# A two-part network in fp32 on one core: layer 0's leftover tiles in one stream with the output planes among its last head pairs, and the even layer's entry rearranged with the low parts of its weights made in halves

## Chip, cores, metric

One core of a Trainium2 chip runs the whole program. The metric is the device time of one execution in microseconds; lower is better.

## What is computed

The reference is a chain of four mixers and two MLPs on 512 tokens of width 1024, all in fp32. Two of the mixers matter here.

```python
def stick_breaking_layer(x, norm_g, w_in, w_out):          # layer 0
    q, k, v, gate = jnp.split(rms_norm(x, norm_g) @ w_in, 4, axis=-1)      # 16 heads of 64
    ...
        z = einsum(q, k) / 8;  mask = s < t
        log_fail = where(mask, log_sigmoid(-z), 0)
        later = cumsum(log_fail, reverse) - log_fail
        a = where(mask, exp(log_sigmoid(z) + later), 0)
    return x + (o * silu(gate)) @ w_out

def even_mixer(h, ...):                                    # the even layer
    qa, ka, va, qi, ki, wi, qb, kvb, gb = split_cols(h @ w_in, EVEN_SPLITS)
    # rope on qa, ka, qi, ki, qb and three of kvb
    o_a = dsa_attention(...)     # 8 heads, keys chosen by an index score (top 128 of up to 512)
    o_b = nsa_attention(...)     # 8 heads: compressed keys (gelu of two small products), selected, window; sigmoid gates
    return concat(o_a, o_b) @ w_out
```

Each matrix is multiplied nearly exactly: both operands are split in a high part (rounded to the fp32r type) and a low part (the rest), and a product is three matmuls, high by high, low by high and high by low.

## The kernel before

**Weights.** SyncE streams blocks of 128x1024 fp32 (512 KB) in the order of a list `plan` into two raw buffers WRAW; ScalarE makes the high part WH (`split_high`, line 252), VectorE or, for the blocks in `on_pool`, GpSimd the low part WL (`split_low`, line 261), in three buffers each (NR, NS = 2, 3). The load of block b (line 243) waits for the low part of block b-2. The high part of block b waits for that load and for the last matmul on block b-3. In the even layer, the blocks in question are in the order e5, wc2(0), wc1(1,2), e6, wc1(1,3), e7, e8, wc2(1), e9, e10, e11, ..., e14, and then e_o; `E_Q` is 7. `split("e", t)` on an engine means the block three places behind e_t: e7 gives e9, e8 gives e10, wc2(1) gives e11, e9 gives e12.

**A tile** is eight "eighths", each of three matmuls of 512 columns (`three`, lines 275 to 277), with its result in one of eight banks of PSUM.

**Layer 0** (`l0_tensor`, `l0_vector`, `l0_scalar`, `l0_gpsimd`) makes gates and values, then the first tiles q0, k0, q1 (`l0_first`), and then goes through eight pairs of heads m. For a pair: `logits(m)` (lines 614 and 620), `values(m-1)` (line 642), eight eighths of tile k(m+1), `sums(2m)` (line 629), four eighths of q(m+2), `sums(2m+1)`, four more. The chain of a head is logits on TensorE; Abs, Exp, Ln on ScalarE (`soft`, lines 775 to 781); `fails` on VectorE (lines 714, 719); `fail_low` on GpSimd (line 822); sums on TensorE; `weigh` on ScalarE (line 787); values. A tile q or k is evicted by VectorE (696), rounded (705), and its low part is GpSimd's (812). The result of a pair goes through `gated` on VectorE (727), `og_zero` on ScalarE (792) and `og_low_zero` on GpSimd (828), and is then an operand of the output product `out_sets`, one "plane" (three matmuls, an eighth of an output tile) per pair. In pair 6 there is one tile left (k7) and in pair 7 none; six planes of output tile 0 stand there before `sums(14)`, one after it, seven planes of tile 1 after `sums(15)`, seven of tile 2 after `values(7)`.

**The even layer** (`l2_tensor`, `l2_vector`, `l2_scalar`, `l2_gpsimd`) makes its first tiles and the compressed keys (the entry) and then goes through 56 steps. In step s TensorE does `turn(s-4)` (line 1607, or 1602 for a compressed unit), `values(s-5)` (1626), `scores(s)` (1583, 1590), perhaps a rotation for rope (1487), and some eighths of the remaining tiles e9 to e14; VectorE does `maxima(s-1)` (1805), `recips(s-3)`, rope, `taken` (eviction, 1726), and rounds of the top-k (`e_rounds`, 1701 and 1703); ScalarE does `copied(s-4)`, `exps(s-1)` (2019), the query's high part (2005) and high parts of weights; GpSimd does `scale(s-3)` (2144), the query's low part `low` (2132), rope's cosine `cos` (2100), and low parts of weights. `scores(s)` needs the banks that `exps(s-2)` frees, `turn(s-4)` needs `scale(s-4)` and banks 4 and 5. Where a tile ends is set by a table of eighths per step, `E_FILL`, that starts in step 2:

```python
        E_FILL0, E_FILL = 2, (1, 2, 1, 1, 2, 1, 0)
        def e_eighths(step):
            s = step - E_FILL0
            return E_FILL[s % 7] if 0 <= s < 42 else 0
```

The order of each engine is that of the code; there is no scheduler.

Of the kernel before, what the change touches and what calls it, by code (L numbers as in the profile page):

```python
# [133 lines left out]
def program(nc, A, out):  # L134
    ctx = ExitStack()
    with ctx:
# [117 lines left out]
        def split_low(e, w, b, pool):  # L254
# [3 lines left out]
            if b >= NS:  # L258
# [3 lines left out]
                            ALU.subtract).then_inc(*inc("s_low_pool" if pool else "s_low", ("low", b)))  # L262

# [307 lines left out]
        l0_first = [("l0q", 0), ("l0k", 0), ("l0q", 1)]  # L571
        l0_beside = [[("l0k", m + 1)] * (m < 7) + [("l0q", m + 2)] * (m < 6) for m in range(8)]

        def l0_tensor(e, w):
# [7 lines left out]
            for name, m in l0_first:  # L582
                tile_t(e, w, name, m, h_hi, h_lo, need)
            w.wait_ge(*at("const", 3))

            def linear(name, m):
# [3 lines left out]
                bank, was = banks.hold((name, m), 7, ("evac", name, m))  # L590
# [4 lines left out]
                for k in range(KT):  # L595
# [4 lines left out]
                    yield  # L600

# [33 lines left out]
            def values(m):  # L635
                o, was = banks.hold(("l0 out", m), 6, ("gated", m))
# [9 lines left out]
            for m in range(8):  # L646
                logits(m)
                if m:
                    values(m - 1)
                tiles = [linear(*t) for t in l0_beside[m]] + [iter(())] * 2  # L650
                if m == 7:
                    out_sets(e, w, "l0o", 0, 0, range(0, 6), 7)
                for _ in range(8):
                    next(tiles[0], None)
                sums(2 * m)
                if m == 7:
                    out_sets(e, w, "l0o", 0, 0, range(6, 7))
                for _ in range(4):
                    next(tiles[1], None)
                sums(2 * m + 1)  # L660
                for _ in range(4):
                    next(tiles[1], None)
            out_sets(e, w, "l0o", 0, 1, range(0, 7), 0)
            values(7)
            out_sets(e, w, "l0o", 0, 2, range(0, 7), 1)
            for m in range(3):
                out_sets(e, w, "l0o", 0, m, [7])
# [3 lines left out]
        def l0_vector(e, w):  # L671
# [27 lines left out]
            def high(name, m):  # L699
# [7 lines left out]
                split_low(e, w, after_block(name, m), False)  # L707
# [13 lines left out]
            def gated(m):  # L721
# [5 lines left out]
                e.tensor_tensor(TMP[:, m % 2, :], BANK[6][:, :], l0g[:, m, :], ALU.mult).then_inc(  # L727
                    *inc("s_gated", ("gated", m)))
            for t in l0_first:
                evicted(*t)  # L730
                high(*t)
            for m in range(8):
                fails(2 * m)
                fails(2 * m + 1, [0])
                beside = l0_beside[m]
# [3 lines left out]
                if m:  # L739
                    gated(m - 1)  # L740
                if len(beside) > 0:
                    high(*beside[0])
                if len(beside) > 1:
                    evicted(*beside[1])
                    high(*beside[1])
            gated(7)
# [2317 lines left out]
```

## Time and profile before

| | us |
|---|---|
| median of 3 runs | 1934.42 (1933.19 to 1934.52) |
| the profiled execution's own time | 1929.6 |
| its span, from the first to the last instruction | 1927.8 |
| TensorE busy in the span | 1847.4 (96%) |
| VectorE, ScalarE, GpSimd busy | 968.3, 796.8, 468.9 |
| mean granted TensorE clock | 0.99 |

Times in rows are from the span's start. "[1.59 <-POOL LH L822]" at the end of a row means that the engine had been idle for 1.59 us and what it waited for last. PEclk is the granted share of TensorE's clock: 1.00 is 2.4 GHz, 0.50 is 1.2 GHz.

### The profile page before, as it was taken

The page shows a single profiled execution, that of the slowest core. Times are in us where ns is not written, and L with a number is a line of the kernel's source. Part 1 is how long each engine was busy: PE and PEld are TensorE (multiplying, and loading weights), DVE is VectorE, ACT ScalarE, POOL GpSimd, SP SyncE. Part 2 cuts the span into 40 slices and gives each one's busy share as a digit, 9 for nine tenths or more (in the row PEclk, how much of TensorE's full clock was granted, in tenths as well). Part 3 has the DMA queues.
Part 4 walks back from the last instruction along what each step waited for, and adds up shares of the span by engine and source line. Part 5 has one row for each costly group of instructions (what it writes and reads, how often), then busy time and mean ns, then how long its engine had stood idle before and what let it go on. Part 6 is the DMA issues. An engine that isn't in the chain of part 4 may idle for free.

```text
span 1927.8 us, 24564 instructions
## 1 busy us (share of the span) xinstructions
PE 1847.4 (96%) x9682; PEld 1452.9 (75%) x9682; DVE 968.3 (50%) x1574; ACT 796.8 (41%) x1401; POOL 468.9 (24%) x467
## 2 busy tenths in 40 slices
PE   6999998999999989999999999999999999999997
PEld 5987776766677746667888888877888788888885
DVE  5355554575545587843543333355555654333334
ACT  4235664355435345554442323133444544232322
POOL 0025551011312125541120102005556312010200
PEclk9999999999999989999999999999999999999998
DMA  4321111221012410001233232322211123323331
GB/s 154 99 77 44 55 45 45 87 77 44 23 45 95 127 55 23 23 23 36 90 105 99 88 98 95 99 79 77 66 55 58 48 94 99 98 88 99 98 99 66
DMA packets 40289, 143.32 MB, mean 74 GB/s; under 512 B 4592, under 2 KB 4976, under 8 KB 40176
## 3 DMA queue, kind: packets, MB, share of 16 engines
q1 hardware_dynamic: 40176, 141.76, 22.7%
q8 instruction: 78, 1.28, 0.3%
q14 instruction: 35, 0.29, 0.0%
HBM read 139.64 MB, written 2.10 MB: 74 GB/s over the span
## 4 chain that ended last, share of the span: by engine, by line
PE 86%; DVE 5%; ACT 4%; POOL 3%; issue 1%; DMA 1%; DVEq 0%; SPq 0%; POOLq 0%; ACTq 0%
PE BANK L275 22%; PE BANK L277 22%; PE BANK L276 22%; PE BANK L856 2%; PE BANK L629 2%; PE BANK L1626 2%; PE BANK L1583 1%; PE BANK L1607 1%; PE BANK L2403 1%; DVE LH L719 1%; PE BANK L913 1%; PE BANK L614 1%; PE BANK L2378 1%; DVE SCR L714 1%; ACT WH L252 1%
## 5 line engine op out<-in xcount | busy, mean ns | idle before, releaser
L252 ACT ACTIVATE WH<-WRAW 128x1024 fp32r<-128x1024 f32 x262 | 273.5, 1045 | 494.9 <-PE BANK L277 458.2
L261 DVE TENSOR_TENSOR WL<-WRAW,WH 128x1024 fp32r<-128x1024 f32 (+1 forms) x249 | 324.9, 1305 | 260.4 <-ACT WH L252 260.2
L275 PE MATMUL BANK<-HH,WH 128*128 128x512 f32 x1048 | 426.9, 407 | 21.1 <-DVE WL L261 18.1
L277 PE MATMUL BANK<-HL,WH 128*128 128x512 f32 x1048 | 410.5, 392 | 0.0
L276 PE MATMUL BANK<-HH,WL 128*128 128x512 f32 x1048 | 410.1, 391 | 0.0
L275 PEld LDWEIGHTS BANK<-HH,WH 128*128 128x128 f32 x1048 | 197.9, 189 | 71.5 <-ACT WH L252 18.8
L276 PEld LDWEIGHTS BANK<-HH,WL 128*128 128x128 f32 x1048 | 198.2, 189 | 43.2 <-issue 5.3
L277 PEld LDWEIGHTS BANK<-HL,WH 128*128 128x128 f32 x1048 | 197.9, 189 | 42.8
L2253 POOL TENSOR_TENSOR HID<-TMP,HID 128x512 fp32r<-128x512 f32 x64 | 83.0, 1297 | 534.2 <-ACT HID L2234 534.2
L277 PE MATMUL BANK<-HID,WH 128*128 128x512 f32 x512 | 202.3, 395 | 0.0
L275 PE MATMUL BANK<-HID,WH 128*128 128x512 f32 x512 | 202.2, 395 | 0.0
L276 PE MATMUL BANK<-HID,WL 128*128 128x512 f32 x512 | 202.2, 395 | 0.0
L463 DVE TENSOR_TENSOR X<-X,BANK 128x512 f32<-128x512 f32 x96 | 66.1, 688 | 251.2 <-PE BANK L277 251.2
L2230 ACT ACTIVATE TMP<-TMP 128x512 f32<-128x512 f32 x64 | 40.5, 632 | 202.8 <-DVE TMP L2207 202.8
L277 PEld LDWEIGHTS BANK<-HID,WH 128*128 128x128 f32 x512 | 96.1, 188 | 23.3
L275 PEld LDWEIGHTS BANK<-HID,WH 128*128 128x128 f32 x512 | 96.1, 188 | 23.3
L276 PEld LDWEIGHTS BANK<-HID,WL 128*128 128x128 f32 x512 | 96.1, 188 | 23.3
L2207 DVE SCALAR_TENSOR_TENSOR TMP<-BANK,RS 128x512 f32<-128x512 f32 x64 | 44.1, 689 | 59.4 <-PE BANK L277 59.4
L812 POOL TENSOR_TENSOR L0P<-TMP,L0P 128x512 fp32r<-128x512 f32 x16 | 36.4, 2276 | 152.6 <-DVE L0P L705 152.6
L822 POOL TENSOR_TENSOR LH<-SCR,LH 128x512 fp32r<-128x512 f32 (+1 forms) x48 | 53.2, 1107 | 45.9 <-DVE LH L719 45.9
L2019 ACT ACTIVATE SCR<-BANK,ST 128x512 f32<-128x512 f32 (+3 forms) x96 | 49.7, 527 | 17.7 <-DVE ST L1805 17.5
L2658 ACT ACTIVATE SCR<-BANK,ST 128x128 f32<-128x128 f32 (+3 forms) x64 | 33.2, 523 | 56.9 <-DVE ST L2529 56.9
(400 smaller groups left out, 3137.5 us busy)
## 6 DMA issues: line engine op xcount, KB each, us to landing
WRAW<-in_w SPq DMA_DIRECT2D x77, 512.0 KB, 3.4
WRAW<-in_wu SPq DMA_DIRECT2D x64, 512.0 KB, 3.3
WRAW<-in_wd SPq DMA_DIRECT2D x64, 512.0 KB, 3.3
WRAW<-in_w0o SPq DMA_DIRECT2D x8, 512.0 KB, 3.5
WRAW<-in_w1o SPq DMA_DIRECT2D x8, 512.0 KB, 3.4
WRAW<-in_wc SPq DMA_DIRECT2D x8, 512.0 KB, 3.4
WRAW<-in_w2o SPq DMA_DIRECT2D x8, 512.0 KB, 3.3
WRAW<-in_w3o SPq DMA_DIRECT2D x8, 512.0 KB, 3.3
```

The lines of the kernel that those rows point to most:

```text
L252: e.activation(WH[b % NS][:, 0:n], WRAW[b % NR][:, 0:n], ACT.Copy).then_inc(*inc("s_high", ("high", b)))
L261: e.tensor_tensor(WL[b % NS][:, 0:n], WRAW[b % NR][:, 0:n], WH[b % NS][:, 0:n].bitcast(F32), ALU.subtract).then_inc(*inc("s_low_pool" if p ...
L275: e.matmul(dst, ah, bh, start=first and i == 0, stop=False)
L276: e.matmul(dst, al, bh, start=False, stop=False)
L277: made = e.matmul(dst, ah, bl, start=False, stop=last and i == len(sets) - 1)
L463: e.tensor_tensor(X[:, m, :], X[:, m, :], banks[name, m], ALU.add).then_inc(*inc("s_evac", ("evac", name, m)))
L629: made = e.matmul(l0_bank(h, bk)[:, c0 + 128 * (jj - j):c0 + size[j]], ntri if jj == j else nones, nlf[:, h % 2, col[jj]:col[jj] + size[jj ...
L822: e.tensor_tensor(LH1[:, h % 2, c], l0_buf[h % 3][:, c], LH0[:, h % 2, c].bitcast(F32), ALU.subtract).then_inc(*inc("s_fail_lo", ("fail lo ...
L2019: e.activation(e_exp(u)[:, b, 0:n], BANK[2 * (u % 2) + b][:, 0:n], ACT.Exp, bias=e_stat(u, b), accum_out=e_stat(u, 2 + b)).then_inc(*inc(" ...
L2207: e.scalar_tensor_tensor(out=TMP[:, t % 4, :], in0=banks[("up", L, c), m], scalar=0.0, in1=RS[:, :], op0=ALU.max, op1=ALU.mult).then_inc(* ...
L2230: e.activation(t, t, ACT.Square).then_inc(*inc("s_hid", ("hid square", L, c, m)))
L2253: e.tensor_tensor(lo[:, m, :], TMP[:, (8 * c + m) % 4, :], hi[:, m, :].bitcast(F32), ALU.subtract).then_inc(*inc("s_hid_lo", ("hid lo", L, ...
```

## The change

In layer 0, q1 is no longer among the first tiles. The tiles from q1 on are one stream of 112 eighths: four before `logits(0)`, twelve in pair 0 before `sums(0)` and eight in the other pairs, and again four after each `sums` (not in pair 6). The output planes start in pair 6 (two after each `sums`), go on in pair 7 with eight before `sums(14)`, two before and two after `sums(15)`, and five after `values(7)`. q1 goes to bank 7, k1 to bank 6, `values(7)` to bank 0, output tiles 0, 1, 2 to banks 7, 6, 1. `gated(6)` and `og_zero(6)` come earlier (before `fails(14)`, and between `soft(14)` and `soft(15)`), `og_low_zero(6)` between `fail_low(14)` and `fail_low(15)`, and the low part of the last pair's result is VectorE's. In the even layer's entry, gelu and the sigmoid of the gates come earlier on ScalarE, rope earlier on VectorE, the low parts of e9, e10 and e11 later there (after `taken(E_Q + 1)`, in step 4 and in step 5), `second(1)` and `c_values` earlier on TensorE. The rope of tile e8 moves from steps 1 and 2 to steps 3 and 4 on VectorE, and no rounds of the top-k are done in steps 0 to 2. The table of eighths starts in step 1 and rests in step 22. In the steps the low part of a block (e12 to e14, e_o 0 to 2) is made by GpSimd in two halves, two and three steps after the tile's end instead of in that step.

```diff
+        def split_low_half(e, w, b, half):
+            n = stream[b][2] // 2
+            c = slice(n * half, n * half + n)
+            w.wait_ge(*at("used", b - NS))
+            w.wait_ge(*at("high", b))
+            e.tensor_tensor(WL[b % NS][:, c], WRAW[b % NR][:, c], WH[b % NS][:, c].bitcast(F32),
+                            ALU.subtract).then_inc(*inc("s_low_pool", ("low", b) if half else ("low half", b)))
...
-        l0_first = [("l0q", 0), ("l0k", 0), ("l0q", 1)]
+        l0_first = [("l0q", 0), ("l0k", 0)]
...
+            tiles = (part for t in [("l0q", 1)] + [t for beside in l0_beside for t in beside] for part in linear(*t))
...
-            for m in range(8):
+            eighths(4)
+            for m in range(6):
                 logits(m)
                 if m:
                     values(m - 1)
-                tiles = [linear(*t) for t in l0_beside[m]] + [iter(())] * 2
-                if m == 7:
-                    out_sets(e, w, "l0o", 0, 0, range(0, 6), 7)
-                for _ in range(8):
-                    next(tiles[0], None)
+                eighths(8 if m else 12)
                 sums(2 * m)
-                if m == 7:
-                    out_sets(e, w, "l0o", 0, 0, range(6, 7))
-                for _ in range(4):
-                    next(tiles[1], None)
+                eighths(4)
                 sums(2 * m + 1)
-                for _ in range(4):
-                    next(tiles[1], None)
-            out_sets(e, w, "l0o", 0, 1, range(0, 7), 0)
+                eighths(4)
+            logits(6)
+            values(5)
+            eighths(8)
+            sums(12)
+            planes(0, 0, 1)
+            sums(13)
+            planes(0, 2, 3)
+            logits(7)
+            values(6)
+            planes(0, 4, 5)
+            planes(1, 0, 1, 2, 3, 4, 5)
+            sums(14)
+            planes(0, 6)
+            planes(1, 6)
+            sums(15)
+            planes(2, 0, 1)
             values(7)
-            out_sets(e, w, "l0o", 0, 2, range(0, 7), 1)
+            planes(2, 2, 3, 4, 5, 6)
...
-        E_FILL0, E_FILL = 2, (1, 2, 1, 1, 2, 1, 0)
+        E_FILL, E_REST = (1, 2, 1, 1, 2, 1, 0), 22
+        def e_place(step):
+            return step - 1 - (step >= E_REST)
...
-            return E_Q + 1 if step == 1 else e_ended(step - 1)
+            return E_Q + 1 if step == 3 else e_ended(step - 1)
...
                 if k == 2:
                     rot_of(E_Q)
-            second(1)
+                if k == 4:
+                    second(1)
+            c_values()
...
             taken(E_Q)
+            after_rope(E_KW)
+            after_rope(E_Q)
+            keys(1)
+            c_keys(1)
+            taken(E_Q + 1)
             split("e", E_Q)
-            after_rope(E_KW)
-            keys(1)
-            after_rope(E_Q)
-            taken(E_Q + 1)
-            split("e", E_Q + 1)
-            c_keys(1)
-            split("wc2", 1)
...
-                if step == 1:
+                if step == 2:
                     index_sum(3)
-                if step == 2:
+                if step == 3:
                     c_values()
+                if step == 4:
+                    split("e", E_Q + 1)
+                if step == 5:
+                    split("wc2", 1)
...
-                for _ in range(1 if busy or step % 2 else 2):
+                for _ in range(0 if step < 3 else 1 if busy or step % 2 else 2):
...
             split("e", E_Q)
-            keys(1)
-            high(E_Q)
             gelu(1)
             e.activation(gates, gates, ACT.Sigmoid).then_inc(*inc("s_gates", ("gates",)))
             e.preload_act_table_set("natural_log_exp_and_others")
+            keys(1)
+            high(E_Q)
+            swapped(1)
             split("e", E_Q + 1)
             split("wc2", 1)
...
-                if e_ended(step) is not None:
-                    split("e", e_ended(step))
+                for half in range(2):
+                    if e_ended(step - 2 - half) is not None:
+                        split_low_half(e, w, block["e", e_ended(step - 2 - half)] + NS, half)
```

The order of instructions moves at these three places. Lines of the changed program differ from those of the one before; the names are the same.

TensorE in pair 6 of layer 0, where `sums(12)` ends and `sums(13)` begins (LH0 and LH1 are the high and low parts of a head's log terms, OG0H and OG0L those of a pair's gated result); before:

```order
L629 MATMUL BANK<-LH0,TRI 128x128
L629 MATMUL BANK<-LH1,TRI 128x128
L629 MATMUL BANK<-LH0,TRI 128x512 [waits s_fail_lo]
L629 MATMUL BANK<-LH1,TRI 128x512
L629 MATMUL BANK<-LH0,TRI 128x384
```

and now:

```order
L643 MATMUL BANK<-LH0,TRI 128x128
L643 MATMUL BANK<-LH1,TRI 128x128
L284 MATMUL BANK<-OG0H,WH2 128x512 [waits s_og_hi,s_evac,s_og_lo,s_low,s_high]
L285 MATMUL BANK<-OG0H,WL2 128x512
L286 MATMUL BANK<-OG0L,WH2 128x512
L284 MATMUL BANK<-OG0H,WH2 128x512 [waits s_og_lo,s_og_hi]
L285 MATMUL BANK<-OG0H,WL2 128x512
L286 MATMUL BANK<-OG0L,WH2 128x512
L643 MATMUL BANK<-LH0,TRI 128x512 [waits s_fail_lo]
L643 MATMUL BANK<-LH1,TRI 128x512
```

Two planes of output tile 0 now stand between the sums of the two heads.

VectorE at the even layer's entry, from `taken(E_Q)` on (WL1<-WRAW0,WH1 is the low part of e9, WL2<-WRAW1 of e10, WL0<-WRAW0 of e11; ekcT is the compressed keys' copy); before:

```order
L1726 SCALAR_TENSOR_TENSOR TMP<-BANK,RS 128x512 [waits s_tile]
L261 TENSOR_TENSOR WL1<-WRAW0,WH1 128x1024 [waits s_high]
L1738 TENSOR_TENSOR TMP<-BANK,ROPE 128x512 [waits s_roped,s_rot]
L1745 TENSOR_TENSOR TMP<-TMP 128x512 [waits s_cos,s_sin]
L1761 TENSOR_TENSOR ekw<-TMP,ekw 128x512 [waits s_key_high]
L1738 TENSOR_TENSOR TMP<-BANK,ROPE 128x512 [waits s_roped,s_rot]
L1745 TENSOR_TENSOR TMP<-TMP 128x512 [waits s_cos,s_sin]
L1726 SCALAR_TENSOR_TENSOR TMP<-BANK,RS 128x512 [waits s_tile]
L261 TENSOR_TENSOR WL2<-WRAW1,WH2 128x1024 [waits s_high]
L1770 COPY ekcT<-BANK 128x62 [waits s_tile]
L261 TENSOR_TENSOR WL0<-WRAW0,WH0 128x1024 [waits s_high]
```

and now:

```order
L1785 TENSOR_TENSOR TMP<-BANK,ROPE 128x512 [waits s_roped,s_rot]
L1792 TENSOR_TENSOR TMP<-TMP 128x512 [waits s_cos,s_sin]
L1785 TENSOR_TENSOR TMP<-BANK,ROPE 128x512 [waits s_roped,s_rot]
L1792 TENSOR_TENSOR TMP<-TMP 128x512 [waits s_cos,s_sin]
L1808 TENSOR_TENSOR ekw<-TMP,ekw 128x512 [waits s_key_high]
L1817 COPY ekcT<-BANK 128x62 [waits s_tile]
L1773 SCALAR_TENSOR_TENSOR TMP<-BANK,RS 128x512 [waits s_tile]
L261 TENSOR_TENSOR WL1<-WRAW0,WH1 128x1024 [waits s_high]
L1852 TENSOR_REDUCE ST<-BANK 128x2 [waits s_scores] x2
```

The low part of e9 moved from the head of this stretch to its end, and the row maxima of steps 1 and 2 follow it at once.

GpSimd around the end of tile e9 in the steps (WL1<-WRAW1,WH1 is the low part of e12); before:

```order
L2144 TENSOR_SCALAR SCR<-SCR,ST,enat 128x256
L261 TENSOR_TENSOR WL1<-WRAW1,WH1 128x1024 [waits s_high,s_tile]
L2144 TENSOR_SCALAR SCR<-SCR,ST,enat 128x384 [waits s_recip]
L2144 TENSOR_SCALAR SCR<-SCR,ST,enat 128x384
L2100 TENSOR_TENSOR TMP<-TMP,ROPE 128x512 [waits s_rot]
```

and now:

```order
L2153 TENSOR_TENSOR TMP<-TMP,ROPE 128x512 [waits s_rot]
L2197 TENSOR_SCALAR SCR<-SCR,ST,enat 128x384 [waits s_recip]
L2197 TENSOR_SCALAR SCR<-SCR,ST,enat 128x384
L2185 TENSOR_TENSOR EQ<-TMP,EQ 128x512 [waits s_query]
L270 TENSOR_TENSOR WL1<-WRAW1,WH1 128x512 [waits s_high,s_tile]
L2197 TENSOR_SCALAR SCR<-SCR,ST,enat 128x128 [waits s_recip]
L2197 TENSOR_SCALAR SCR<-SCR,ST,enat 128x128
L270 TENSOR_TENSOR WL1<-WRAW1,WH1 128x512
```

The low part stood ahead of the cosine; it now comes behind the query's low part, in two pieces with a unit's scaling between them.

## Rows read from the trace of the kernel before

**Rows 1.** The page: its first line.
```profile
span 1927.8 us, 24564 instructions
```
**Rows 2.** Windows: us; busy (instructions) of PE, PEld, DVE, ACT, POOL; PEclk; DMA; GB/s.
```profile
113.00:128.00 15.00, 15.00 (x67) 12.39 (x66) 5.93 (x8) 2.78 (x3) 4.58 (x2) 1.00 0.28 87
300.52:303.93 3.41, 2.88 (x7) 2.42 (x8) 0.00 (x0) 0.29 (x2) 0.39 (x1) 0.50 0.00 0
699.88:716.94 17.06, 11.67 (x45) 6.61 (x42) 14.35 (x35) 6.39 (x15) 3.20 (x3) 0.50 0.19 62
717.20:906.00 188.80, 177.19 (x1454) 127.40 (x1454) 112.15 (x265) 101.15 (x263) 84.82 (x113) 0.99 0.06 18
809.10:812.50 3.40, 3.40 (x26) 2.57 (x24) 3.37 (x8) 1.39 (x4) 0.66 (x1) 0.50 0.23 92
```
**Rows 3.** Waits of PE, 275 to 322 us: total, times, longest.
```profile
PE BANK L629 <- POOL LH L822: 3.2, 3, 1.6
PE BANK L275 <- POOL OG0L L828: 3.2, 1, 3.2
PE BANK L614 <- ACT SCR L787: 1.8, 1, 1.8
```
**Rows 4.** Timeline of PE in layer 0: start, duration, instruction [idle before].
```profile
129.93 2.20 PE L614 MATMUL BANK<-L0P 64*128 64x512 f32 x24 [1.09 <-DVE TMP L696]
141.01 2.99 PE L629 MATMUL BANK<-LH,TRI 128*128 128x512 f32 x20 [2.79 <-POOL LH L822]
```
**Rows 5.** Timeline of POOL and DVE in layer 0.
```profile
124.67 2.29 POOL L812 TENSOR_TENSOR L0P<-TMP,L0P 128x512 fp32r<-128x512 f32 x1 [3.15 <-DVE L0P L705]
...
290.40 0.43 DVE L719 CAST LH<-SCR 128x512 fp32r<-128x512 f32 x1
...
291.46 1.03 DVE L719 CAST LH<-SCR 128x512 fp32r<-128x512 f32 x1
...
298.38 0.73 POOL L822 TENSOR_TENSOR LH<-SCR,LH 128x256 fp32r<-128x256 f32 x1 [0.23 <-DVE LH L719]
299.64 1.26 POOL L828 TENSOR_TENSOR OG0L<-TMP,OG0H 128x512 fp32r<-128x512 f32 x1 [0.53 <-ACT OG0H L792]
```
**Rows 6.** Waits of PE at the even layer's entry, 687 to 717.2 us.
```profile
PE BANK L275 <- POOL EHL L2124: 1.8, 1, 1.8
...
PE BANK L1487 <- DVE TMP L1738: 0.6, 1, 0.6
```
**Rows 7.** Timeline of PE there.
```profile
708.87 1.33 PE L1583 MATMUL BANK<-eks,EQ 64*128 64x384 f32 x6 [4.51 <-ACT SCR L2019]
...
717.19 1.31 PE L1607 MATMUL BANK<-CF,SCR 128*128 128x128 f32 x8
```
**Rows 8.** Timeline of DVE and ACT there.
```profile
696.46 0.69 DVE L1726 SCALAR_TENSOR_TENSOR TMP<-BANK,RS 128x512 f32<-128x512 f32 x1 [0.22 <-PE BANK L277]
701.79 1.23 DVE L261 TENSOR_TENSOR WL<-WRAW,WH 128x1024 fp32r<-128x1024 f32 x1 [4.64 <-ACT WH L252]
...
706.03 1.22 DVE L1805 TENSOR_REDUCE ST<-BANK 128x2 f32<-128x1024 f32 x1
...
700.70 2.00 ACT L252 ACTIVATE WH<-WRAW 128x1024 fp32r<-128x1024 f32 x2
```
**Rows 9.** The weight loads of line 243, 690 to 710 us: issue to landing.
```profile
DMA to landing us min/median/max: 3.5/3.5/5.3
```
**Rows 10.** Waits of PE in the steps, 717.2 to 906 us.
```profile
PE BANK L1607 <- POOL SCR L2144: 6.7, 8, 1.7
PE BANK L1602 <- DVE SCR L1841: 2.7, 1, 2.7
```
**Rows 11.** Timeline of POOL in the steps.
```profile
755.20 2.35 POOL L261 TENSOR_TENSOR WL<-WRAW,WH 128x1024 fp32r<-128x1024 f32 x1 [1.68 <-ACT WH L252]
```
**Rows 12.** Groups of DVE's instructions by line, 717.2 to 906 us: busy, mean ns.
```profile
L1701 DVE MAX8 ST<-esc 128x8 f32<-128x384 f32 (+2 forms) x33 | 20.1, 610 | 0.2
L1703 DVE MATCH_REPLACE8 esc<-ST,esc 128x384 f32<-128x384 f32 (+2 forms) x33 | 19.9, 603 | 0.0
```

More of the change, by code:

```diff
@@ L583, in l0_tensor @@
                 tile_t(e, w, name, m, h_hi, h_lo, need)
+            banks.i += 1
             w.wait_ge(*at("const", 3))
@@ L589, in linear @@
                 wh, wl = (x[b % NS][:, 0:BW].rearrange("p (k n) -> p k n", k=KT) for x in (WH, WL))
-                bank, was = banks.hold((name, m), 7, ("evac", name, m))
+                bank, was = banks.hold((name, m), 6 if (name, m) == ("l0k", 1) else 7, ("evac", name, m))
                 w.wait_ge(*at("high", b))
@@ L600, in linear, with planes @@
                     yield
+            def planes(m, *ks):
+                for k in ks:
+                    out_sets(e, w, "l0o", 0, m, [k], (7, 6, 1)[m])
             def logits(m):
@@ L635, in values @@
             def values(m):
-                o, was = banks.hold(("l0 out", m), 6, ("gated", m))
+                o, was = banks.hold(("l0 out", m), 0 if m == 7 else 6, ("gated", m))
                 for key in was:
@@ L645, in values, with eighths @@
                 made.then_inc(*inc("s_o", ("o", m)))
-            for m in range(8):
+            tiles = (part for t in [("l0q", 1)] + [t for beside in l0_beside for t in beside] for part in linear(*t))
+            def eighths(n):
+                for _ in range(n):
+                    next(tiles)
+            eighths(4)
+            for m in range(6):
                 logits(m)
@@ L731, in l0_vector @@
                 high(*t)
+                split_low(e, w, after_block(*t), False)
+            evicted("l0q", 1)
+            high("l0q", 1)
             for m in range(8):
+                beside = l0_beside[m]
+                if m == 7:
+                    gated(6)
                 fails(2 * m)
                 fails(2 * m + 1, [0])
-                beside = l0_beside[m]
                 if len(beside) > 0:
@@ L1671, in l2_tensor @@
                     scores(step)
-                if e_turning(step) is not None:
+                if step == 1:
+                    rot_of(E_Q + 1)
+                elif step > 3 and e_turning(step) is not None:
                     rot_of(e_turning(step), (7,))
-                if step == 2:
-                    c_values()
                 for _ in range(e_eighths(step)):
@@ L2065, in l2_scalar @@
             keys(0)
+            swapped(0)
             split("wc1", 1, 3)
```

48 lines of the change are left out of this document (27 added, 21 removed).

## The prediction, made before the changed kernel ran

> **What bounds the kernel now.** I read the page first. The span is 1927.8 us [rows 1] and TensorE is busy in 96% of it, so it is TensorE's order that sets the end, and the change adds and removes no product. Time can come only from TensorE's waits and from stretches in which its granted clock is halved. Second, I took TensorE's waits by what ended them, in the three stretches whose order changes. From 275 to 302 us the reader sees three chains end last: the sums wait for GpSimd's low part of the log terms (3.2 us in 3 waits), the output planes for its low part of the gated result (3.2), the logits for `weigh` on ScalarE (1.8) [rows 3]. Two more stand at the start of layer 0: 1.09 before `logits(0)` and 2.79 before `sums(0)` [rows 4]. At the even layer's entry it waits 1.8 for gelu's low part and 0.6 for the rotated query [rows 6], then 4.51 for `exps(0)` [rows 7]; in the steps 6.7 for `scale` and 2.7 for a chain on VectorE [rows 10]. Third, windows show the clock. It is 0.50 in three stretches of 3.41, 17.06 and 3.40 us, where TensorE is busy 2.88, 11.67 and 3.40; half of each is lost, so 1.4, 5.8 and 1.7 us [rows 2]. In that table 67 matmuls fill 15.00 us at full clock, 0.224 each, so an eighth or a plane is 0.68. The stakes are these waits and losses, some 31 us, in a program whose other 1895 stand as they are.
>
> **Layer 0, its start: 2.6 us saved.** Before, k0's tile ended and 24 matmuls of q1 (5.4 us) covered its eviction, rounding and low part; 1.09 of it stood open. Now 12 cover it (2.7). k0's low part begins at 124.67 and takes 2.29 [rows 5], to 126.97, while TensorE, by its pitch, runs out near 126.0, so `logits(0)` waits about 1.0. `sums(0)` came 11.08 us after the start of `logits(0)` (141.01 less 129.93, [rows 4]), which is the length of that head's chain; 2.20 of logits and now 36 matmuls (8.1) instead of 24 stand beside it, 10.3, with small gaps 10.8, and I take 0.3 of wait. Waits go from 3.88 to 1.3. The splits that move behind `soft(1)` and `fails(1)` are wanted a pair later and cost nothing; without that pair of cover they would cost a low part of GpSimd, 2.29.
>
> **Layer 0, its end: 7.3 us saved.** The waits are 3.2, 3.2 and 1.8 [rows 3]; of the first, 0.3 belongs to `sums(12)` and stays, so 7.9 are at stake. Two planes (1.36) now stand before `sums(13)` and cover its 1.3. Twelve matmuls more before `values(6)` and `sums(14)` leave, I estimate, 0.4 and 0.2 of the 1.8 and 1.6. The 3.2 before the planes of pair 6 goes: `og_low(6)` is made early and planes of other pairs stand ahead. New waits come instead. `sums(15)` needs a low part that ended at 299.11 (298.38 and 0.73 [rows 5]); now `og_zero` stands ahead on ScalarE and `og_low` (1.26 [rows 5]) on GpSimd, and the casts of VectorE take 1.03 rather than 0.43 beside GpSimd's work [rows 5]; I take 300.3 and 1.1 of wait, and 0.3 at `values(7)`. That leaves 2.0, so 5.9 are saved. With no wait of 3.2 the stretch at half clock behind it goes, 1.4.
>
> **The even layer's entry: 8.0 us saved, 6 to 10.** Times here are on the scale of before, without what layer 0 saves. The low part of e9 leaves VectorE's path before the rope, so the wait of 0.6 for the rotated query goes; gelu comes before the keys on ScalarE, so the 1.8 goes too [rows 6]. Tile e8 then ends near 696.3 and `scores(0)` can start about 2 us earlier. But the low part of e9 now follows e8's eviction (0.69 [rows 8]): it runs from 697.0 to 698.3 (1.23 [rows 8]). The load of e11 goes into the buffer that this low part frees, so it is issued at 698.3 and lands 3.5 later [rows 9], at 701.8; its high part (2.00 for two, so 1.0 [rows 8]) stands ahead of `exps(0)` on ScalarE. Hence `exps(0)` near 702.9. Before, it followed the maxima that ended at 707.25 (706.03 and 1.22 [rows 8]), and `scores(2)` came 1.6 later, at 708.87 [rows 7]; now it comes at 704.5. TensorE idles about 3.6 before it, one wait where there were four. From 708.87 to `turn(0)` at 717.19 [rows 7] are 8.3, 0.9 of them idle, 7.4 busy at half clock: 3.7 at full. I add 1.7 for one stretch of half clock of the size of the one at 809.10 [rows 2], which gives `turn(0)` at 709.9, 7.3 earlier, with one eighth (0.7) more behind it: 8.0. The ends: if e11 lands at once, 10; if it takes the 5.3 of the slowest load [rows 9], 6.
>
> On whether the new wait halves the clock, rows do not agree: after the wait of 2.79 at 141.01 [rows 4] no half stretch stands in the trace, after the 2.7 near 809 [rows 10] one does [rows 2]. The Trainium skill (TensorE: Matmul & The Clock Gate, on the HAM clock gate) says that the gate looks at the engine in a rhythm of its own, not the program's; by that the 1.7 that I add is a throw, and the sum would be 25.1 without it.
>
> **The steps: 5.5 us saved, 0 to 11.** Here 6.7 and 2.7 us of waits [rows 10] and 1.7 of clock are at stake, 11.1. GpSimd waited 1.68 for the block's high part and then worked 2.35 on the whole low part [rows 11], with `scale` and the cosine queued behind. The halves come two and three steps later, when the high part is long made, and take about half each (nearest row: a GpSimd operation of 128x512 at 1.26 [rows 5]); by rows the two are 2.5, 0.2 dearer than the whole. Loads of later blocks wait two to three steps more, some 7 to 10 us, and have the rest of a tile as cover. What is late next: from a rotation's end the chain cosine (1.3), roped (0.7), high (0.65), query's low (1.3), a half (1.3) and scale (up to 1.5) is 6.7 us, against two steps of 3.4 each (188.80 over 56 [rows 2]). That is a tie, so some waits stay. VectorE is the other doubt: a round is 0.61 and 0.60 and small parts, about 1.4 us [rows 12], and those of steps 0 to 2, some five, are done later, beside the low parts of e10 and e11 (1.2 each) in steps 4 and 5. I take the middle of nothing and all, 5.5; a loss is the rival below.
>
> **The sum.** 2.6 + 7.3 + 8.0 + 5.5 = 23.4. The profiled execution took 1929.6, so 1906.2; the median of the runs is 1934.42, 4.8 above it, so 1911.0.
>
> **The rivals.** All on the median's scale; 0.2% of it, 3.9 us, is about what a measurement of this kernel can tell from no change.
>
> *More is gained.* The clock stays full at the entry (1.7) and all waits of the steps go (5.6 more): 30.7, 1903.7. For it: 2.79 of wait once left the clock alone. Against: the tie on GpSimd. Chance 0.12.
>
> *VectorE's later rounds take the gain of the steps.* Five rounds and two low parts are 9.6 us of VectorE moved into steps in which it also frees banks; if they cost the 5.5, 1916.5. For it: the 2.7 near 809 came from VectorE's chain [rows 10]. Against: VectorE is busy 112 of 188.80 us [rows 2]. Chance 0.11.
>
> *The halves stand in the way.* The 5.5 are not saved, and in two of six tiles a half (1.3) delays `scale` besides: 8.1 less, 1919.1. Chance 0.06.
>
> *The entry gains nothing.* The load of e11 and what follows it hold `exps(0)` until 707 or a later bank is late: 8.0 and a bit less, 1919.0 at the nearest. Chance 0.06.
>
> *It doesn't do what it says,* or several shortfalls meet, and it stays within 0.2%. Chance 0.04.
>
> *Slower.* The clock falls in the new wait of 3.6 at the entry and does not rise in the steps, whose matmuls are short and broken by waits. Each busy us at half clock costs half of itself; to undo 23.4 and 3.9 more it must be half for 55 us (27.3 by 2), which gives 1938.3. Before, the longest such stretch here was 17.06, with waits of 4.51 and 0.9 inside it [rows 2, 7]; the point from which it decides is three times that. Chance 0.03.
>
> **How the numbers follow.** The forecast has 0.58 and a range of its own of 1906 to 1916, from 6 to 10 at the entry and from 2 to 9 in the steps. To 1903.5 below and 1921 above the range takes in all rivals but the last two and leaves out some of the forecast's tails. Faster by over 0.2%: 0.93; within: 0.04; slower: 0.03.
>
> **What would show it right or wrong.** In layer 0: waits of about 1.0 and 0.3 before `logits(0)` and `sums(0)`, no wait over 0.5 before `sums(15)`, about 1.1 there, and clock 1.00 throughout. At the entry: one wait of 3 to 4 us before `scores(2)`, ended by `exps(0)`, with a high part that waited for a load just ahead of it on ScalarE; `turn(0)` 7.3 us earlier than before, besides the 9.9 of layer 0, so near 700 us. In the steps: `turn` waits for `scale` between 0 and 4 us in all, and none of `scores` for VectorE. I am wrong if `exps(0)` waits for the maxima again, if the half clock lasts beyond 7 us, or if new waits of over 1 us on evictions or maxima stand in the first ten steps.

## The result, and the profile after

The changed kernel takes 1916.38 us, the median of 4 runs (1915.41 to 1919.55), beside 1933.81 (1928.79 to 1934.52) for the kernel before, whose three runs have a fourth beside them here. The ratio is 0.9918, interval 0.9898 to 0.9939: some 16 us faster, or 0.8%. The forecast was 1911.0, with a range of 1903.5 to 1921. The profiled execution took 1915.41 and its span is 1913.6, against 1929.6 and 1927.8 [rows 1], so the traces differ by 14.2 us. Layer 0 and the entry came out close to their terms; the steps, which were to give 5.5, lost 1.6.

The page's first lines:

```profile
span 1913.6 us, 24565 instructions
## 1 busy us (share of the span) xinstructions
PE 1842.6 (96%) x9678; PEld 1450.0 (76%) x9682; DVE 967.3 (51%) x1575; ACT 796.1 (42%) x1401; POOL 471.0 (25%) x472
```

**Layer 0.** Waits of TensorE from 275 to 313.5 us, beside [rows 3]:

```profile
PE BANK L643 <- POOL LH L862: 1.3, 2, 1.1
PE BANK L284 <- DVE WL L261: 1.2, 1, 1.2
PE BANK L628 <- ACT SCR L823: 0.3, 1, 0.3
```

The 3.2 before pair 6's planes is gone. Of the sums' waits those of 1.31 and 1.59 are gone and one of 1.05 has come, before `sums(15)`; 0.22 stands before `sums(14)`. The 0.33 before `sums(12)` is as it was, but ends at 273.11, just outside this window, where it was inside before. The 1.8 before the logits is 0.3. The 1.2 on a weight's low part stood there before too, at 321.61 us of the old trace; it ends at 312.48 now, so 9.1 us are won by then. The two waits at the start, from the timeline of TensorE, beside [rows 4]:

```profile
126.91 0.51 PE L628 MATMUL BANK<-L0P 64*128 64x512 f32 x2 [0.97 <-POOL L0P L852]
139.38 0.50 PE L643 MATMUL BANK<-LH,TRI 128*128 128x512 f32 x1 [1.45 <-POOL LH L862]
```

The first is as forecast (1.0), the second is 1.45 where 0.3 was expected.

**The entry.** ScalarE's timeline shows what holds `exps(0)` (its first row is L2070), and TensorE's the wait for it:

```profile
687.90 1.06 ACT L252 ACTIVATE WH<-WRAW 128x1024 fp32r<-128x1024 f32 x1
691.92 1.06 ACT L252 ACTIVATE WH<-WRAW 128x1024 fp32r<-128x1024 f32 x1 [2.96 <-DMA WRAW<-in_w]
692.88 0.67 ACT L2070 ACTIVATE SCR<-BANK,ST 128x512 f32<-128x512 f32 x1
```
```profile
694.45 0.44 PE L1628 MATMUL BANK<-eks,EQ 64*128 64x384 f32 x2 [3.60 <-ACT SCR L2070]
699.74 0.27 PE L1652 MATMUL BANK<-CF,SCR 128*128 128x128 f32 x1
```

ScalarE idled 2.96 us for the load of e11 with its high part, and `exps(0)` stood behind it. `turn(0)` comes 387.26 us after layer 0's last wait; before, it was 395.58 (717.19 less 321.61), so 8.3 are won on this way. Some 0.7 of it is not the entry's: a wait of 1.28 at 652.12 of the old trace, ahead of the entry, is 0.58 here, and it is absent in the run below that has the old code there.

**The steps and the clock.** Waits of TensorE from `turn(0)` to just before the exit, beside [rows 10], and windows over the stage and over the two stretches at half clock that are left between the start and the end of the program (columns as in [rows 2]):

```profile
PE BANK L1652 <- POOL SCR L2197: 8.4, 7, 2.5
PE BANK L1647 <- DVE SCR L1888: 2.0, 1, 2.0
PE BANK L1652 <- ACT EPB L2086: 1.2, 2, 1.0
PE BANK L1632 <- issue: 0.6, 4, 0.2
PE BANK L1652 <- ACT MORE L2086: 0.3, 1, 0.3
```
```profile
696.00:699.41 3.41, 3.41 (x14) 2.29 (x14) 3.15 (x12) 1.23 (x4) 2.70 (x3) 0.50 0.01 2
699.70:889.60 189.90, 175.10 (x1446) 124.88 (x1448) 117.16 (x279) 100.20 (x262) 88.48 (x119) 1.00 0.07 23
890.57:893.98 3.41, 3.41 (x9) 2.63 (x8) 3.32 (x5) 2.11 (x4) 0.00 (x0) 0.50 0.68 244
```

From `turn(0)` to the output product are 189.8 us, with no us at half clock; before they were 188.3, of which 1.7 was lost to the clock. The waits grew from 9.0 to 11.7 (those over 0.28 us each). By the table of eighths, one eighth (0.7) of the stage's work now comes ahead of `turn(0)`, so at equal work the steps lost some 2.3. The second stretch follows the wait of 1.78 at the exit, which stood there before without one: 1.7 more. The account of the two spans: 9.1 and 8.3 won, 1.6 and 1.7 given back, 14.1 of 14.2.

### The profile page after: what moved, and what is told of

It reads as the page before. It is cut to its first block, busy times and chain, and to the rows that moved or that the text cites. A ratio compares the mean times of both kernels' runs of the same rounds, so it can differ in the third digit from the quotient of the medians.

```text
span 1913.6 us, 24565 instructions
## 1 busy us (share of the span) xinstructions
PE 1842.6 (96%) x9678; PEld 1450.0 (76%) x9682; DVE 967.3 (51%) x1575; ACT 796.1 (42%) x1401; POOL 471.0 (25%) x472
## 3 DMA queue, kind: packets, MB, share of 16 engines
q8 instruction: 78, 1.28, 0.3%
## 4 chain that ended last, share of the span: by engine, by line
PE 87%; DVE 5%; ACT 3%; POOL 3%; issue 2%; DMA 1%; DVEq 0%; SPq 0%; POOLq 0%; ACTq 0%
PE BANK L284 22%; PE BANK L286 22%; PE BANK L285 22%; PE BANK L897 2%; PE BANK L643 2%; PE BANK L1652 1%; PE BANK L1671 1%; PE BANK L1628 1%; PE BANK L2454 1%; PE BANK L954 1%; PE BANK L628 1%; PE BANK L2429 1%; DVE LH L745 1%; POOL LH L862 1%; DVE WL L261 1%
## 5 line engine op out<-in xcount | busy, mean ns | idle before, releaser
L2197 POOL TENSOR_SCALAR SCR<-SCR,ST,enat 128x512 f32<-128x512 f32 (+3 forms) x64 | 41.1, 651 | 61.9 <-DVE ST L1874 61.7
```

The lines of the kernel that those rows point to most:

```text
L2197: e.tensor_scalar(x, x, e_stat(u, 4 + b), gate, ALU.mult, ALU.mult).then_inc(*inc("s_scaled", ("e scaled", u, b)))
```

## The experiments

Three theories stood against each other for the steps. The forecast's own: the low part of the weights on GpSimd makes turn wait, and halving it helps. The second: the halves stand in the way where they are put. The third: other moves of the change (VectorE's rounds, the table of eighths) took the gain. For each run I compare the stage from `turn(0)` to the exit by its idle time (TensorE's waits over 0.28 us, without the exit's own 1.8) and by its time at half clock, since the second changes the time by more than most edits do.

**Layer 0 alone** (`l0_only`): all of the diff up to layer 0's end on the kernel before.

> The kernel before with the layer 0 part of the change alone. In the changed kernel's profile the last wait of layer 0 ends 9.1 us earlier than before (312.5 against 321.6). Theory (the parts are independent): the same waits as in the changed kernel (about 1.0 before logits(0), 1.4 before sums(0), 1.1 before sums(15)), the even layer as before (a wait of 4.5 before scores(2), turn(0) 395.6 after that last wait), so the span falls by 9 us. Rival (the even layer's waits depend on when its loads come): the entry or the steps change by more than 2 us although their code is that of before.

Measured: 1920.03 median (ratio 0.9945, 0.9928 to 0.9962), span 1916.8, 11.0 less than before. Layer 0's last wait ends at 312.75. The steps take 188.27 us, as before, with the same seven waits, the two largest of them 2.7 and 1.7. From layer 0's last wait to `turn(0)` it took 394.38 rather than 395.58: the wait of 1.28 at 652.12 of the old trace is not there. The parts are independent to about 1 us, less than the 2 that the rival asked for; the rest of the change gives the other 3 to 5.

**The low part whole, at the tile's end** (`low_whole`), **and whole, two steps later** (`low_whole_late`):

```diff
-                for half in range(2):
-                    if e_ended(step - 2 - half) is not None:
-                        split_low_half(e, w, block["e", e_ended(step - 2 - half)] + NS, half)
+                if e_ended(step) is not None:
+                    split("e", e_ended(step))
```

The second run has `e_ended(step - 2)` in both new lines.

> The changed kernel, but GpSimd makes each low part of e12 to e_o whole, in the step in which the tile ends, as before. Theory 1 (the halves help, and something else took the gain of the steps): the stage from turn(0) to the exit, 189.8 us in the changed kernel, gets longer by 2 to 4 us, with waits of turn for scale of 0.7 to 1.7 just behind each tile's end, and the span grows as much. Rival (the halves are what stands in the way, since each comes just ahead of a scale): the stage gets shorter by 1 to 4 us, and the wait of 2.5 (850.75) goes.

> The changed kernel, but the low part is made whole two steps after the tile's end. It tells the moving from the halving. If the moving alone helps, the stage from turn(0) to the exit is within 1 us of that of the changed kernel (189.8). If halving is what matters, each of six low parts of 2.35 us stands ahead of a scale, about 1.1 us more than a half does, and the stage gets longer by 3 to 7 us, with waits of turn for scale of 2 to 3.5. If the halves are in the way only by their number, the stage gets shorter.

Measured: 1920.23 (0.9944, 0.9929 to 0.9959) and 1920.85 (0.9950, 0.9935 to 0.9965). Idle in the steps was 12.5 and 15.1 against 11.7 in the changed kernel; the time at half clock there 17.1 and 13.7 us against none. With `low_whole` the wait of 2.5 at 850.75 goes, as its rival said, but others of 0.6 to 1.8 come at the tiles' ends, as its theory said; neither had the net of 0.8 more idle. Halves at this place thus save 0.8 of waits against the old form and 3.4 against a whole low part at the same place. It looked as if halving mattered; the next two runs say otherwise. Waits in the steps with the whole low part two steps later:

```profile
PE BANK L1652 <- POOL SCR L2197: 11.8, 9, 3.6
```

**The halves one step later** (`halves_34`): `step - 3 - half` in place of `step - 2 - half`. **The whole low part at three steps** (`whole_3`): `split("e", e_ended(step - 3))`.

> The changed kernel, but the two halves of a low part come three and four steps after the tile's end, not two and three. Theory (a half stands ahead of a unit's scale in the same step in which the query's low part is made, so turn waits there: 1.6 at 770.9 and 2.5 at 850.8): those two fall by 0.4 and 1.2 or more, no wait is added elsewhere, and the idle time of the steps falls from 11.7 to about 10. Rival (the blocks' loads and high parts come a step later and the next tile waits for its weights, or the half meets another late scale): waits of a tile's first product for a weight appear, or the idle time of the steps stays within 0.5 of 11.7.

> The changed kernel with the low part made whole three steps after the tile's end. It tells halving from placing, beside the kernel with halves at three and four steps (idle 9.3 in the steps) and that with the whole low part at two (15.1). If the place is what matters, the idle time is 9 to 10.5. If halving matters at any place, since 2.35 us stand ahead of a scale that is already due, it is 11.5 to 15, with waits of 1.5 to 2.5 three steps behind the tiles' ends.

Measured: 1910.30 (0.9886, 0.9858 to 0.9913) and 1911.72 (0.9894, 0.9880 to 0.9909), both below the changed kernel's 1916.38, though the intervals of the ratios still touch its own (0.9898 to 0.9939); the waits are clearer. GpSimd's timeline about the longest wait, first in the changed kernel, then with the halves one step later:

```profile
847.55 1.27 POOL L2185 TENSOR_TENSOR EQ<-TMP,EQ 128x512 fp32r<-128x512 f32 x1 [2.31 <-ACT EQ L2056]
848.78 1.26 POOL L270 TENSOR_TENSOR WL<-WRAW,WH 128x512 fp32r<-128x512 f32 x1
850.02 1.15 POOL L2197 TENSOR_SCALAR SCR<-SCR,ST 128x384 f32<-128x384 f32 x2
```
```profile
846.40 1.27 POOL L2185 TENSOR_TENSOR EQ<-TMP,EQ 128x512 fp32r<-128x512 f32 x1 [2.31 <-ACT EQ L2056]
847.65 1.14 POOL L2197 TENSOR_SCALAR SCR<-SCR,ST 128x384 f32<-128x384 f32 x2
```

The query's low part came late, since ScalarE's high part did; the half (L270) behind it pushed the scale (L2197) 1.26 further, and TensorE's wait was 2.49 instead of 1.27. The waits in the steps are the same with halves and with the whole, here of `halves_34` and `whole_3`:

```profile
PE BANK L1652 <- POOL SCR L2197: 6.0, 7, 1.3
PE BANK L1647 <- DVE SCR L1888: 2.0, 1, 2.0
```
```profile
PE BANK L1652 <- POOL SCR L2197: 6.0, 7, 1.3
PE BANK L1647 <- DVE SCR L1888: 2.0, 1, 2.0
```

Idle is 9.3 in both. So the place is what matters: halving is worth 3.4 at two steps, where a half or a whole stands ahead of a late scale, and nothing at three.

**The high part of e11 behind `exps(0)`** (`high_later`):

```diff
             split("e", E_Q + 1)
-            split("wc2", 1)
...
                     exps(step - 1)
+                if step == 1:
+                    split("wc2", 1)
```

> The changed kernel, but on ScalarE the high part of e11 comes in step 1 behind exps(0), not ahead of step 0. Theory (exps(0) waits for the load of e11 only because that high part stands ahead of it): maxima(0) ended at 689.8, so exps(0) starts at about 690 instead of 692.9, the wait of 3.6 before scores(2) falls to 0.7 or less, no half clock follows (1.7), turn(0) comes 4 to 4.6 earlier. Rival (the next wait takes its place: recips, the second bank, or exps(1) behind the high part, which still waits for the load until 691.9): turn(0) comes less than 2 us earlier, with a new wait of PE within the first three steps. The steps behind are either shifted as they are, or take up to 2 us back.

Measured: 1913.47 (0.9908, 0.9893 to 0.9923). `exps(0)` starts at 688.76, the wait before `scores(2)` is 0.58 and not 3.60, no half clock follows, and `turn(0)` comes 383.00 after layer 0's last wait, 4.3 earlier. That part is as the theory said. Two waits of 0.94 and 1.08 for `turn` came in the first steps, and 13.7 us at half clock stood in the stage: one stretch just behind the wait of 1.6 that ends at 767.07 and one from inside the wait of 2.5 that ends at 849.74, both of which had left the clock alone in the changed kernel. The two stretches here (only 0.6 us of waiting is inside), then two windows as long about the same waits in the changed kernel (3.4 us of waiting inside):

```profile
767.20:774.00 6.80, 6.80 (x30) 4.86 (x31) 3.38 (x9) 2.07 (x6) 3.76 (x6) 0.50 0.24 81
849.10:855.90 6.80, 6.17 (x25) 4.27 (x25) 1.03 (x2) 1.51 (x5) 4.04 (x7) 0.50 0.24 81
```
```profile
767.00:773.80 6.80, 5.16 (x45) 3.50 (x42) 6.20 (x16) 3.45 (x11) 6.23 (x8) 1.00 0.03 8
849.00:855.80 6.80, 5.05 (x44) 3.60 (x45) 1.03 (x2) 2.93 (x10) 5.65 (x8) 1.00 0.26 82
```

TensorE issued 55 matmuls here and 89 there in as much time, though it waited longer there. 13.7 us at half clock cost 6.8 at the most; the clock, and the two new waits, took what the entry gave, and the span is only 0.9 shorter. The ratio does not tell this run from the changed kernel; the gain shows in the trace alone.

**The table of eighths as before** (`table_two`): `return step - 2` in place of `return step - 1 - (step >= E_REST)`. **The rounds put back** (`rounds_early`): the 0 rounds of steps 0 to 2 become two, one, two.

> The changed kernel with the table of eighths started in step 2 and without the rest in step 22, as before (the halves still come two and three steps after a tile's end). Theory (the shift put a closing unit, whose result ScalarE copies out, and a rotation into one step without eighths: waits of 1.0 on the exponents' copy at 766 and 1.6 behind it): those two fall to the 0.8 to 1.5 that stood in that place before, and the idle time of the steps falls by 1 to 2 us. Rival (the shift was worth its price): waits of 1 us or more appear in the first ten steps or near 743, and the idle time stays or grows.

> The changed kernel with the top-k rounds of steps 0 to 2 put back (two, one and two). Theory (VectorE's later rounds delay the maxima and so recips, which scale then waits for: 1.2 at 740.8, 0.7 at 762.2, 1.0 at 797.1): turn(0) comes 1 to 3 us later, and the idle time of the steps falls by 1.5 to 3 us. Rival (the rounds are short against a step wherever they stand, and those waits come from the order cosine, low part, maxima itself): the steps' waits stay within 0.5 us of 11.7 and only the entry is later.

Measured: 1913.80 (0.9905, 0.9872 to 0.9938) and 1919.38 (0.9930, 0.9902 to 0.9958). With the old table idle in the steps is 10.0 instead of 11.7 (the 1.0 and 1.6 near 766 become 0.8; two of 0.65 appear early), as the theory said, but the entry's wait is 4.28 and not 3.60, since an eighth that covered it is gone. The two together are 14.3 with the old table and 15.3 with the new, so the shift mostly moves waits and costs 1.0. With the rounds put back idle in the steps is 13.2 and `turn(0)` comes 0.6 later, not 1 to 3: new waits of 0.6 and 1.2 stand at the start, and of the three blamed on late rounds none is shorter (1.20, 0.93 and 1.01 for 1.2, 0.7 and 1.0); only the 0.6 at 807, which was not among them, went. That theory falls, and so does its rival, which had the steps unchanged.

**q1's eviction behind `fails(0)`** (`q1_after`):

```diff
-            evicted("l0q", 1)
-            high("l0q", 1)
             for m in range(8):
...
                 fails(2 * m)
+                if m == 0:
+                    evicted("l0q", 1)
+                    high("l0q", 1)
...
                 fail_low(2 * m)
+                if m == 0:
+                    low("l0q", 1)
```

> The changed kernel, but q1's eviction and rounding come behind fails(0) on VectorE and its low part behind fail_low(0) on GpSimd. Theory (sums(0) waits 1.45 because q1's eviction holds the first log term for 0.8 and GpSimd's low part of q1 beside it makes the casts 1.03 rather than 0.43): the wait before sums(0) falls to 0.3 or less, and the last wait of layer 0 ends about 1.2 us earlier against the wait before logits(0). Rival (the casts are slow beside any GpSimd work, and fail_low is such work): it falls by 0.7 only, to 0.7. The steps of the even layer stay as they are but for the clock.

Measured: 1915.38 (0.9911, 0.9883 to 0.9939). VectorE's timeline in the changed kernel shows why `sums(0)` waited: q1's eviction and rounding (L723, L732) come first, and the log term's cast (L745) is slow while GpSimd makes q1's low part (133.76 to 135.06):

```profile
132.53 0.69 DVE L723 SCALAR_TENSOR_TENSOR TMP<-BANK,RS 128x512 f32<-128x512 f32 x1 [6.88 <-PE BANK L286]
133.25 0.43 DVE L732 CAST L0P<-TMP 128x512 fp32r<-128x512 f32 x1
133.59 0.69 DVE L740 SCALAR_TENSOR_TENSOR SCR<-BANK,SCR 128x512 f32<-128x512 f32 x1
134.31 1.03 DVE L745 CAST LH<-SCR 128x512 fp32r<-128x512 f32 x1
```

With the edit no wait over 0.28 is left before `sums(0)`, but `sums(1)` waits 1.05, because q1's low part now stood ahead of `fail_low(1)`. The waits are 0.4 less, and in time nothing is won: layer 0's last wait ends 185.54 after the start of `logits(0)`, and 185.57 in the changed kernel. That is neither what the theory nor what the rival gave.

**The moves together** (`best_a`, `best_b`): halves at three and four steps, e11's high part behind `exps(0)`, q1's eviction behind `fails(0)` and its low part behind `fail_low(1)`; `best_b` with the old table besides.

> The changed kernel with three moves together: halves three and four steps after a tile's end, the high part of e11 in step 1 behind exps(0), and q1's eviction behind fails(0) with its low part behind fail_low(1). If their gains add: the waits before sums(0) and sums(1) 0.4 at most (1.0 to 1.5 saved), turn(0) 3 to 4.3 earlier besides, idle in the steps 9.3 and 2 for the waits of 0.9 and 1.1 that come in the first two steps. At full clock that is 1.2, 3.5 and 1.5, so 6 less than the changed kernel's span, which by its own stretches at half clock comes out 2 to 8 us faster, near 1909. Rival (the shorter entry wait is given back at turn(0) and turn(1), where VectorE's and GpSimd's chains are late): less than 2 us below the kernel with the halves at three and four steps alone (1910.3).

> The same with the table of eighths as before (start in step 2, no rest). In the steps the waits of 1.0 and 1.6 near 766 gave way to one of 0.8, and two of 0.65 came near 705 and 720: idle 10.0 against 11.7. With the halves moved, 1.2 more goes at the tile's end that had 2.5. I expect idle in the steps 0 to 1 below that of the kernel with the shifted table, so both within 1.5 us of each other at equal clock. Rival: without an eighth in step 1 TensorE waits longer for the first scale, and it is 1 us slower.

Measured: 1907.66 (1906.88 to 1908.00; 0.9873, 0.9856 to 0.9889) and 1907.46 (0.9872, 0.9857 to 0.9886). Their intervals lie below that of the changed kernel. The waits at the start of layer 0 in `best_a`:

```profile
PE BANK L628 <- POOL L0P L853: 1.0, 1, 1.0
PE BANK L643 <- POOL LH L863: 0.4, 1, 0.4
```

The edits add: 1.0 less of waits in layer 0 (0.6 of it in time, from `logits(0)` to the last wait), 3.7 us less up to `turn(0)`, idle in the steps 11.0 (9.3 and the two waits that the earlier start brings). `best_a` has 3.4 us at half clock where the changed kernel has 6.8. It is 2.6 below `halves_34` alone, where its rival asked for less than 2. Idle in the steps of `best_b` is 9.4 and its entry waits longer; in time the two tables are equal.

**The new place under the old entry** (`old_entry_whole_3`): `l0_only` with the whole low part three steps after the tile's end, in the even layer's code of before.

> The kernel with the layer 0 part of the change alone, whose even layer is that of before, but each whole low part of e12 to e_o is made three steps after the tile's end. It shows what the place of the low part is worth under the entry and the table of before. If the waits of turn for scale in the old steps (0.3, 1.7, 0.8, 0.7, 1.5 and 1.3, six of them) all come from the low part at the tile's end, idle in the steps falls from 9.0 to 3 to 5, with the 2.7 behind VectorE's chain left, and the shift of e8's rope, the rounds and the table then cost the changed kernel some 5 us. Rival (most of them come from the query's chain of cosine, sine, high and low part, whatever the low part of the weights does): it falls by less than 3, to 6 to 9, and the changed kernel's other moves cost little.

Measured: 1916.77 (0.9930, 0.9911 to 0.9949). Waits in the steps, beside [rows 10]:

```profile
PE BANK L1639 <- POOL SCR L2176: 5.6, 6, 1.3
PE BANK L1634 <- DVE SCR L1873: 2.3, 2, 2.0
```

Idle falls from 9.0 to 8.0 only, as the rival said, but only in part for the rival's reason. The old trace has the whole low part right ahead of the late scale at five of the eight waits for `scale`, 5.0 of the 6.7 us. Here is the one of 1.5, TensorE's row and GpSimd's:

```profile
859.77 0.30 PE L1607 MATMUL BANK<-CF,SCR 128*128 128x128 f32 x1 [1.50 <-POOL SCR L2144]
```
```profile
856.60 2.36 POOL L261 TENSOR_TENSOR WL<-WRAW,WH 128x1024 fp32r<-128x1024 f32 x1 [4.08 <-ACT WH L252]
858.93 1.36 POOL L2144 TENSOR_SCALAR SCR<-SCR,ST 128x512 f32<-128x512 f32 x2
```

Turn by turn, the waits of 1.70, 0.83, 0.71 and 1.50 at these places are 0.95, 0.12, 0 and 0 once the low part is moved, and the 2.70 behind VectorE's chain is 1.98: 4.4 us less. But 3.5 us come at other turns, mostly one or two later: 0.79 for 0.31, and new ones of 0.36, 0.79, 1.01 and 0.83. No low part stands ahead in these. The 0.36 is VectorE's own; in the others GpSimd's scale had waited for VectorE's reciprocals (L1859), as in the second 0.79:

```profile
777.08 0.30 PE L1639 MATMUL BANK<-CF,SCR 128*128 128x128 f32 x1 [0.79 <-POOL SCR L2176]
```
```profile
775.92 1.66 POOL L2176 TENSOR_SCALAR SCR<-SCR,ST,enat 128x384 f32<-128x384 f32 x2 [1.52 <-DVE ST L1859]
```

VectorE had gone from 773.07 to 775.66 without a break through a query's rope product, a top-k round and a row maximum before these reciprocals. The waits for the low part had hidden a chain on VectorE that was nearly as late. No run here takes the round or the maximum out of its way.

## Why the prediction was right, and where not

**The number.** The forecast was 1906.2 for the profiled execution, which took 1915.41: 9.2 more. On the median the miss is 5.4, because 4.8 was added for the distance from that execution to the median and the changed kernel's is 1.0. This is luck. The measured 1916.38 lies just outside the forecast's own range of 1906 to 1916, and inside the wide one because that takes in the rivals. In the traces the parts come to 1.5 + 7.7 + 8.3 - 1.6, less 1.7 for a half clock at the exit, where 23.4 were forecast. The waits and losses listed at the head of the prediction add up to 37.3 us, not to some 31; no term was made from that figure.

**Layer 0, start: 2.6 forecast, 1.5 measured.** The wait before `logits(0)` was right (0.97 for 1.0). The wait before `sums(0)` was 1.45 for 0.3. The step that failed is "`sums(0)` came 11.08 us after the start of `logits(0)`": I took the chain's length as fixed, and the change put q1's eviction into its middle. It measured 12.47 (139.38 less 126.91). The moved eviction was costed at nothing; I had looked at the splits and not at it. The run `q1_after` shows that it is the cause of this wait; taking it away there only made the next sum wait.

**Layer 0, end: 7.3 forecast, 7.7 measured.** 6.3 of waits and 1.4 of clock, no half clock in the layer. The new wait before `sums(15)` is 1.05 for 1.1, that before the logits 0.30 for 0.4, that before `sums(14)` 0.22 for 0.2, and the 0.3 at `values(7)` did not come. Taken together with the start, 9.9 were forecast and 9.1 are seen at the layer's last wait.

**The entry: 7.3 earlier forecast, 8.3 measured.** Every step is in the trace: low part of e9 at 687.22, load issued at 688.47, high part at 691.92, `exps(0)` at 692.88, a wait of 3.60 for 3.6, one stretch of 3.41 at half clock. `turn(0)` came at 699.74 for "near 700". Of the 1.0 beyond the forecast, 0.7 is the shorter wait ahead of the entry. `high_later` shows that the high part's place on ScalarE was the cause of the wait that is left, as the chain said. That the waits of 1.8 and 0.6 went for the reasons given is seen in the trace; no run tests them one by one.

**The steps: 5.5 forecast, a loss of 1.6 measured.** By the forecast's own sign `turn` was to wait between 0 and 4 us for `scale`; it waited 8.4. The step that failed is the first sentence of that part, that 6.7 and 2.7 us of waits "are at stake" for the low part. The row with GpSimd's low part of 2.35 ahead of a scale [rows 11] was read rightly, and four more of the eight waits look like it. What failed is the step from there to the gain: a wait was taken to be worth its length. `old_entry_whole_3` measured what the low part's place is worth: 4.4 less at these waits and at VectorE's, 3.5 more at others, 1.0 in all. VectorE was taken up as a doubt for its later rounds and low parts; its reciprocals, nearly as late as the low part, were not followed. The tie worked out for the query's chain on GpSimd was right, and a half adds 1.26 to it where it is longest: two halves out of twelve, 2.4 of waits (`halves_34`).

That is the rival of the halves in the way, which had a chance of 0.06. It put the steps at a loss of 2.6; measured are 1.6, or 2.3 at equal work. For the profiled execution its terms give 1914.3, 1.1 from what was measured; on the median, with the 4.8 named above, its 1919.1 is 2.7 off. Its halves are true (2.4), but that the 5.5 did not come is not their doing. The rival of VectorE's later rounds has the nearest number, 1916.5, and its mechanism is refuted by `rounds_early`: that is chance too. What remains (9.3 of idle in `halves_34` against 8.0 with the old entry) comes with the shifted table and the other moves. `table_two` gives 1.7 of idle back in the steps and takes 0.7 at the entry; the other parts I leave open.

**The clock.** At the entry the 1.7 that I added came. I did not forecast one at the exit. The wait of 1.78 there is the same in all 13 traces of this study beside that of before, and half clock follows it in two of them, the changed kernel's being one. The Trainium skill (TensorE: Matmul & The Clock Gate, on the HAM clock gate) has the gate look in a rhythm of its own; the traces agree so far, with the same waits of 1.6 and 2.5 followed by no half clock in one kernel and by 13.7 us of it in another. The rival of a slower kernel was never near: the most half clock in the steps of any run was 17.1 us, where 55 was the point from which it decides.

## What to carry to other kernels

Before costing the removal of a wait, look at what comes next behind the suspect: when the late instruction's other inputs were ready, and how late the next turn's are. A wait is worth its length only down to the second-latest chain; here 4.4 us went and 3.5 came back. When an operation is moved into another engine's chain, even one of 0.7 us, follow that chain to who waits for it, and prefer to change its place over cutting it up. A filling instruction that waits for a load belongs behind the work that is due, as e11's high part showed with 4.3 us.

## What was not expected of the hardware

A small VectorE instruction took seven times as long beside GpSimd as alone (168 and 172 ns). The gates' product with the reciprocals, 128x8 elements, runs four times in the steps; durations in ns, least, median and most:

```profile
L1885 DVE TENSOR_TENSOR ST<-ST,enat x4: 168/206/1209, 724.3 to 823.0; 128x8 f32<-128x8 f32 x4
```

The slow one ran from 791.16 to 792.37, while GpSimd made a cosine:

```profile
791.09 1.26 POOL L2153 TENSOR_TENSOR TMP<-TMP,ROPE 128x512 f32<-128x512 f32 x1 [4.14 <-PE BANK L1532]
```

It ended as the cosine did (792.35). The fourth, of 239 ns, ran from 823.03 beside the last 0.22 us of a scale and ended with it too. So do two in the old trace, of 943 and 905 ns: they end within 0.03 us of the end of GpSimd's instruction beside them. For this product what is lost is the rest of GpSimd's instruction. It is not so for every small one: the reciprocal of 128x8 just ahead of it (L1882) took 203 ns beside the scale at 822.80 and 202 alone.

That is 1.0 of the wait of 1.98 at 792.98, which no run here removed. Keeping the cosine out of that step would be the next thing to try; it wasn't tried. And two halves of a low part (1.26 and 1.27) cost GpSimd 0.2 more than the whole (2.35), as the rows had said, and bought nothing at three steps.
